# Expert mixtures: the down product turned around, with rounded splits for the sample tokens and four column groups for the prompt tokens

## The reference

```python
def expert_choice_moe(h, w_router, w_gate, w_up, w_down):
    ...
    gates, idx = lax.top_k(aff.T, cap)
    xe = t[idx]
    hid = jax.nn.silu(jnp.einsum('ecd,edf->ecf', xe, w_gate)) * jnp.einsum('ecd,edf->ecf', xe, w_up)
    ye = jnp.einsum('ecf,efd->ecd', hid, w_down) * gates[..., None].astype(h.dtype)
    out = jnp.zeros_like(t).at[idx.reshape(-1)].add(ye.reshape(-1, d))
```

## Time and profile before

| | us |
|---|---|
| median of 3 runs | 4536.19 (4535.85 to 4536.8) |
| the profiled execution, its own time | 4531.31 |
| its span, first to last instruction | 4529.7 |
| PE busy in the span | 3930.1 (87%) |
| the three product groups of the mixtures (lines 1390 and 1413), PE busy | 524.4 + 517.5 + 515.6 |

### The profile page before, as it was taken

The page is one execution under the profiler, slowest core; times in us unless marked ns, Lnnn a source line. Parts: engine busy times, 40 slices in busy tenths (PEclk is TensorE's granted clock), DMA queues, the critical chain, the costliest instruction groups (busy, mean ns, idle before and its releaser), DMA issues. The chain is left out here.

```text
span 4529.7 us, 63871 instructions
## 1 busy us (share of the span) xinstructions
PE 3930.1 (87%) x25037; PEld 3363.6 (74%) x25037; DVE 1418.3 (31%) x2316; ACT 918.4 (20%) x1867; POOL 532.1 (12%) x560
## 2 busy tenths in 40 slices
PE   8689999986899999995999996688599359999996
PEld 1468989864499999994999992344355359999996
DVE  0233433335311111112203437688543531111111
ACT  1223333322110111103222220233221201111111
POOL 0000000020000100002110016333200000001100
PEclk9799999987899999995999998899799579999998
DMA  6200000035688778852212238433432447887775
GB/s 233 77 13 10 8 9 8 4 108 220 237 278 281 269 246 279 279 167 78 78 52 78 79 96 358 166 125 125 186 143 93 163 166 246 279 278 276 261 258 195
DMA packets 351387, 736.85 MB, mean 163 GB/s; under 512 B 24381, under 2 KB 78098, under 8 KB 338642
## 3 DMA queue, kind: packets, MB, share of 16 engines
q1 hardware_dynamic: 315728, 627.98, 38.6%
q0 software_dynamic: 21920, 73.15, 5.8%
q10 hardware_dynamic: 13666, 34.74, 2.0%
HBM read 636.83 MB, written 98.99 MB: 162 GB/s over the span
## 5 line engine op out<-in xcount | busy, mean ns | idle before, releaser
L1390 PE MATMUL banks<-moe_xT,mix_wg 128*128 128x144 f32 x4096 | 524.4, 288 | 5.5 <-DVE moe_xT L1459 1.9
L1390 PEld LDWEIGHTS banks<-moe_xT,mix_wg 128*128 128x128 f32 x4096 | 511.6, 191 | 13.8 <-issue 13.7
L1390 PE MATMUL banks<-moe_xT,mix_wu 128*128 128x144 f32 x4096 | 517.5, 286 | 0.0
L1413 PE MATMUL banks<-moe_hid,moe_wd 128*128 128x144 f32 x4096 | 515.6, 287 | 2.0 <-DVE moe_hid L1466 2.0
L1390 PEld LDWEIGHTS banks<-moe_xT,mix_wu 128*128 128x128 f32 x4096 | 508.2, 190 | 0.0
L1413 PEld LDWEIGHTS banks<-moe_hid,moe_wd 128*128 128x128 f32 x4096 | 505.3, 190 | 3.8 <-DVE moe_hid L1466 2.4
L1466 DVE TENSOR_TENSOR moe_hid<-moe_sg,banks 128x432 f32<-128x432 f32 (+1 forms) x96 | 53.2, 554 | 950.9 <-ACT moe_sg L1437 950.9
L1437 ACT ACTIVATE moe_sg<-banks 128x432 f32<-128x432 f32 (+1 forms) x96 | 47.1, 490 | 903.6 <-PE banks L1390 903.6
L1329 POOL DMA_INDIRECT res<-moe_y_s,moe_id_s x32 | 51.9, 1622 | 1396.7 <-DVE moe_y_p L1478 1396.7
L97 PE MATMUL banks<-h_hi,conv_w_hi 128*128 128x384 f32 x576 | 195.0, 339 | 11.6 <-DVE conv_w_lo L1851 10.8
L1473 DVE TENSOR_TENSOR moe_ye<-banks,modc 128x384 f32<-128x384 f32 (+1 forms) x192 | 59.7, 352 | 449.5 <-PE banks L1413 449.5
(11 more groups left out here) (354 smaller groups left out, 6559.1 us busy)
## 6 DMA issues: line engine op xcount, KB each, us to landing
mix_wg<-in_moe_w_gate SPq DMA_DIRECT2D x64, 2048.0 KB, 7.9
mix_wu<-in_moe_w_up SPq DMA_DIRECT2D x64, 2048.0 KB, 12.9
moe_wd<-in_moe_w_down SPq DMA_DIRECT2D x64, 2048.0 KB, 9.2
start_m_w<-in_w_mod SPq DMA_DIRECT2D x12, 2048.0 KB, 9.5
topk_m_w<-in_w_mod SPq DMA_DIRECT2D x12, 2048.0 KB, 9.2
states_x<-d_xs SPq DMA_DIRECT2D x18, 1024.0 KB, 9.8
d_hin<-states_h ACTq DMA_DIRECT2D x18, 1024.0 KB, 8.0
ssd_hin<-d_hin SPq DMA_DIRECT2D x18, 1024.0 KB, 9.8
```

Of the source, the lines that this page charges most:

```text
L1390: last = pe.matmul(PS[:, bank, CAP * (f - a):CAP * (f - a + 1)], w[:, f // 4, k, P * (f % 4):P * (f % 4) + P], xT[:, k, :], start=(k == 0) ...
L1413: last = pe.matmul(PS[:, q, CAP * (f - a):CAP * (f - a + 1)], wd[:, f // 4, k, P * (f % 4):P * (f % 4) + P], hid[:, k, :], start=(k == 0), ...
```

## The change

Only the down product and what hangs on it change; gate and up stay. Per expert:

- The down product is turned around: activations are stationary and weights move, so the result has tokens on partitions at once, and `rows_back` and `ye` go.
- Sample tokens: 48 matmuls by `exact_products`, 512 columns moving, two banks. ACT rounds the down weights into `wd_hi` (`rounded_down`, four pieces of 128x2048) and the hidden values into `hid_hi`; POOL makes `wd_lo` (`rest_of_down`, four pieces, between its gather and its scatter), DVE makes `hid_lo` (`rest_of_hidden`).
- Prompt tokens: 32 float32 matmuls (eight contraction steps, four column groups `j`). The stationary operand is the 16 tokens, held twice (32 columns); group `j` writes PSUM partitions 32j to 32j + 31 with 256 of the 1024 output features.
- The gates are multiplied in when DVE empties PSUM, from `g2s` and `g2p`, which ten matmuls make once per layer.
- Prompt rows travel as 128 pieces of 512 B in place of 16 rows of 4 KB; `choose` makes their indices with nine more small DVE operations. One transpose replaces the eight small ones.
- `y_s` now lies in `sg`, `y_2` in `hid_p`. The down weights of the next expert are loaded once the prompt products have read them (`p_mm`) and POOL has made the remainders (`dlo_ok`).
- The bias of the modulation is loaded by SP inside `Modulation`, once per layer, in place of ACT at the start.

```diff
+        rows_p = st.sb("rows_p", [NE, KD, CAP_P])
...
+                for k in range(KD):
+                    dve.tensor_scalar(rows_p[:, k], rows[:, CAP_S:CAP], float(KD), float(k), ALU.mult, ALU.add).then_inc(picked, 1)
...
         wd = st.sb("wd", [P, 2, KD, HB])
+        wd_hi, wd_lo = st.sb("wd_hi", [P, 2, KD, HB], F32R), st.sb("wd_lo", [P, 2, KD, HB], F32R)
...
-        x_p = st.sb("x_p", [CAP_P, D])
+        x_p = st.sb("x_p", [P, P])
...
+        id_p = st.sb("id_p", [P, 2], U32)
...
         sg = st.sb("sg", [P, KD, CAP])
-        hid = st.sb("hid", [P, KD, CAP])
-        ye = st.sb("ye", [P, KD, CAP])
-        y_s = st.sb("y_s", [P, D])
-        y_p = st.sb("y_p", [CAP_P, D])
+        hid_hi, hid_lo = st.sb("hid_hi", [P, KD, CAP_S], F32R), st.sb("hid_lo", [P, KD, CAP_S], F32R)
+        hid_p = st.sb("hid_p", [P, KD, 2, CAP_P])
+        y_s = sg[:].rearrange("p k c -> p (k c)")[:, 0:D]
+        y_2 = hid_p[:].rearrange("p k u c -> p (k u c)").rearrange("p (i n) -> p i n", i=2)
+        y_p = st.sb("y_p", [P, P])
+        g2s = st.sb("g2s", [P, D])
+        g2p = st.sb("g2p", [P, 2, P])
...
+        normed_p = g.normed.rearrange("t (k p) -> (t k) p", p=P)
+        res_p = g.res.rearrange("t (k p) -> (t k) p", p=P)
...
-                        sp.wait_ge(half_d if half == 0 else d_mm, e if half == 0 else 3 * e)
+                        sp.wait_ge(p_mm, e)
+                        sp.wait_ge(dlo_ok, 4 * e - 2 + 2 * half)
                         load_down(e, half)
...
-                    pool.indirect_dma_start(x_p[:], None, g.normed, bass.IndirectOffsetOnAxis(ap=id_p[:, 0:1], axis=0),
...
+                    pool.indirect_dma_start(x_p[:], None, normed_p, bass.IndirectOffsetOnAxis(ap=id_p[:, 0:1], axis=0),
...
-                    wait_alone(pool, ys_ok, 2 * e + 2)
-                    pool.indirect_dma_start(g.res, bass.IndirectOffsetOnAxis(ap=id_s[:, 1:2], axis=0), y_s[:], None,
+                    wait_alone(pool, ys_ok, 2 * e + 3)
+                    pool.indirect_dma_start(g.res, bass.IndirectOffsetOnAxis(ap=id_s[:, 1:2], axis=0), y_s, None,
...
                     wait_alone(pool, yp_ok, e + 1)
...
+                                            bounds_check=KD * T - 1, compute_op=ALU.add).then_inc(yp_out, 16)
+                def rest_of_down(e):
+                    for n in range(4):
+                        half, ks = n // 2, slice(4 * (n % 2), 4 * (n % 2) + 4)
+                        wait_alone(pool, dhi_ok, 4 * e + n + 1)
+                        pool.tensor_tensor(wd_lo[:, half, ks], wd[:, half, ks], wd_hi[:, half, ks].bitcast(F32),
+                                           ALU.subtract).then_inc(dlo_ok, 1)
...
                         gather(e + 1, 4 * e + 2)
+                        rest_of_down(e)
                         scatter(e, 4 * e + 4)
                     else:
+                        rest_of_down(e)
                         scatter(e, 4 * e + 2)
...
+                    pe.transpose(PS[:, 3, 0:P], x_p[:], g.ident[:]).then_inc(x_mm, 1)
+                pe.sem_inc(d_mm, 1)
+                pe.wait_ge(g2_in, 3)
+                for k in range(KD):
+                    pe.matmul(PS[:, k // 4, P * (k % 4):P * (k % 4) + P], sg[:, k, 0:P], g.ident[:], start=True, stop=True)
+                picks = hid_p[:].rearrange("p k u c -> p (k u c)")
...
+                tokens(0, 0)
...
+                            if bank < 2:
+                                pe.wait_ge(ys_ok, 2 * e + bank)
...
-                        tokens(e + 1, 2 * e, 3 * e + 1)
+                        tokens(e + 1, 3 * e + 1)
                     pe.wait_ge(hid_ok, 3 * e + 3)
-                    for q, (a, b) in enumerate(TRIOS):
...
+                    for half in range(2):
+                        pe.wait_ge(wd_in[half], 16 * e + 16)
+                    for k in range(KD):
+                        for j in range(4):
+                            last = pe.matmul(PS[32 * j:32 * j + 32, 4, 0:256], hid_p[:, k].rearrange("p u c -> p (u c)"),
+                                             wd[:, j // 2, k, 256 * (j % 2):256 * (j % 2) + 256],
+                                             start=(k == 0), stop=(k == KD - 1))
+                    last.then_inc(p_mm, 1)
+                    pe.wait_ge(hlo_ok, 3 * e + 3)
+                    for half in range(2):
+                        for k in range(KD):
+                            if k % 4 == 0:
+                                pe.wait_ge(dlo_ok, 4 * e + 2 * half + k // 4 + 1)
+                            last = exact_products(pe, PS[:, half, :], (hid_hi[:, k], hid_lo[:, k]), (wd_hi[:, half, k], wd_lo[:, half, k]),
+                                                  k == 0, k == KD - 1)
                         last.then_inc(d_mm, 1)
...
+                def rounded_down(e, half):
+                    act.wait_ge(wd_in[half], 16 * e + 16)
+                    act.wait_ge(d_mm, 2 * e + half)
+                    for k0 in (0, 4):
+                        act.copy(wd_hi[:, half, k0:k0 + 4], wd[:, half, k0:k0 + 4]).then_inc(dhi_ok, 1)
+                def rounded_hidden(e, q):
+                    a, b = TRIOS[q]
+                    act.wait_ge(hid_ok, 3 * e + q + 1)
+                    act.copy(hid_hi[:, a:b], sg[:, a:b, 0:CAP_S]).then_inc(hhi_ok, 1)
                 tokens(0)
                 def body(e, more):
                     for q, (a, b) in enumerate(TRIOS):
+                        if q < 2:
+                            rounded_down(e, q)
                         act.wait_ge(gu_mm, 3 * e + q + 1)
+                        if q == 0:
+                            act.wait_ge(ys_out, 16 * e)
                         act.activation(sg[:, a:b], trio(q, a, b), ACT.Silu).then_inc(sg_ok, 1)
+                        if q:
+                            rounded_hidden(e, q - 1)
+                    rounded_hidden(e, 2)
                     if more:
                         tokens(e + 1)
...
-                        act.activation(y_s[:, 512 * half:512 * half + 512], PS[:, 6 + half, :], ACT.Copy,
-                                       scale=g.gate_s[:, bass.ds(e, 1)]).then_inc(ys_ok, 1)
...
+                gates = g.modc[:, layer, 40:48]
+                dve.sem_inc(ys_ok, 1)
+                dve.tensor_copy(sg[:, :, 0:P], gates[:, :, 1:2].to_broadcast([P, KD, P])).then_inc(g2_in, 1)
...
+                dve.wait_ge(g2_mm, 1)
+                dve.tensor_copy(g2s[:].rearrange("p (t n) -> p t n", t=2), PS[:, 0:2, :]).then_inc(g2_ok, 1)
+                dve.tensor_copy(g2p[:], PS[:, 2, 0:2 * P].rearrange("p (i n) -> p i n", i=2)).then_inc(g2_ok, 1)
...
                 tokens(0)
+                def rest_of_hidden(e, q):
+                    a, b = TRIOS[q]
+                    dve.wait_ge(hhi_ok, 3 * e + q + 1)
+                    dve.tensor_tensor(hid_lo[:, a:b], sg[:, a:b, 0:CAP_S], hid_hi[:, a:b].bitcast(F32), ALU.subtract).then_inc(hlo_ok, 1)
                 def body(e, more):
                     for q, (a, b) in enumerate(TRIOS):
                         dve.wait_ge(sg_ok, 3 * e + q + 1)
-                        dve.tensor_tensor(hid[:, a:b], sg[:, a:b], trio(3 + q, a, b), ALU.mult).then_inc(hid_ok, 1)
+                        up = trio(3 + q, a, b)
+                        dve.tensor_tensor(hid_p[:, a:b], sg[:, a:b, CAP_S:CAP].unsqueeze(2).to_broadcast([P, b - a, 2, CAP_P]),
+                                          up[:, :, CAP_S:CAP].unsqueeze(2).to_broadcast([P, b - a, 2, CAP_P]), ALU.mult)
+                        dve.tensor_tensor(sg[:, a:b, 0:CAP_S], sg[:, a:b, 0:CAP_S], up[:, :, 0:CAP_S], ALU.mult).then_inc(hid_ok, 1)
+                        if q:
+                            rest_of_hidden(e, q - 1)
+                    rest_of_hidden(e, 2)
                     if more:
                         tokens(e + 1)
-                    for q, (a, b) in enumerate(TRIOS):
...
-                                              ALU.mult).then_inc(ye_ok, 1)
...
+                    dve.wait_ge(p_mm, e + 1)
+                    dve.scalar_tensor_tensor(out=y_2, in0=PS[:, 4, 0:2 * P].rearrange("p (i n) -> p i n", i=2),
+                                             scalar=g.gate_p[:, bass.ds(e, 1)], in1=g2p[:], op0=ALU.mult, op1=ALU.mult).then_inc(y2_ok, 1)
...
                     dve.wait_ge(yp_out, 16 * e)
...
-                                      g.gate_p[:, bass.ds(e, 1)], None, ALU.mult).then_inc(yp_ok, 1)
+                    dve.tensor_tensor(y_p[:], y_2[:, 0], y_2[:, 1], ALU.add).then_inc(yp_ok, 1)
+                    dve.wait_ge(ys_out, 16 * e)
+                    for half in range(2):
+                        dve.wait_ge(d_mm, 2 * e + half + 2)
+                        c = slice(HB * half, HB * half + HB)
+                        dve.scalar_tensor_tensor(out=y_s[:, c], in0=PS[:, half, :], scalar=g.gate_s[:, bass.ds(e, 1)],
+                                                 in1=g2s[:, c], op0=ALU.mult, op1=ALU.mult).then_inc(ys_ok, 1)
```

(18 more changed lines are left out.)

80 lines of the change are left out of this document (27 added, 53 removed).

## The result

The changed kernel takes 4425.12 us (median of 4 runs, 4421.04 to 4427.07) against 4536.49 us: a ratio of 0.9753, with an interval of 0.9741 to 0.9765. The forecast was no change, 4538 us, so it was wrong, and the time lies 3 us outside the range too. What happened is rival 1, which had put 4438 us.

What follows compares the result with a forecast made beforehand. The tensor engine's queue was taken as the bound; the new tail's terms, 1.37 + 7.2 + 10.9 + 0.1 = 19.6 us against 19.56 a turn, plus 1 us once per layer, gave 4538 us, range 4428 to 4570.

Steps and rivals of the forecast that it cites:

- rival 1: Prompt matmuls: all four column groups stream at once, 4.1 us in place of 7.2, 4438 us in all; chance 0.30.
- (b): The 32 prompt matmuls: two records side by side at most, one record's time per matmul, 7.2 us a turn.
- The lower bound: Prompt matmuls: the issue rate, 0.064 us a record, so 64 records need at least 4.1 us.
- (c): The 48 rounded products of 512 columns: 0.227 us each as in the attention's output, 10.9 us a turn.
- (a): From the start of the token transposes until the down product may begin: 1.37 us, against 1.57 before.
- (d): The edge from one turn of the expert loop to the next: 0.1 us.
- Once per layer: Gate matmuls, index operations in `choose`, last evacuation and bias loads: together about +1 us, bounds -3 to +5.
- Rival 3: Prompt matmuls: weight loads are not covered, 10.2 us for the block, 4633 us in all; chance 0.06.
- Rival 4: Down-weight remainders: POOL is late, a turn grows by up to 1 us, up to 4570 us; chance 0.06.
- partial overlap: The prediction's own case for the prompt matmuls: two streams at most, 4524 to 4552 us; chance 0.44.
- full overlap: Prompt matmuls of all four column groups stream at once, 4438 us; chance 0.30.

Runs made afterwards that it cites:

- runs: The changed kernel with the prompt matmuls ordered by column group, all sixteen records of a group in a row: 4675.3 us.
- half_turns: The changed kernel with the prompt product on bfloat16 views, one record per matmul instead of two: 4342.6 us.
- ahead: The changed kernel with `hid_hi` and `hid_lo` allocated ahead of `wd` in SBUF instead of behind it: 4414.2 us.
- one_group: The changed kernel with all 32 prompt matmuls in column group 0, three quarters of the prompt result not computed: 4755.1 us.

## Why the prediction was wrong

- **(b), the prompt block: the step that failed.** "so the second has to wait for the first, and the next group's first record stands behind it." The second does wait, but in its own group's queue, and the next group's first record starts past it. That "a record starts when the one ahead has streamed" was read from rows in which all matmuls went to the same columns; there it could not be otherwise, and it said nothing on other groups. 3.59 us instead of 7.2 is 116 us over 32 turns, a little more than the whole miss of 113 us (4538 − 4425). The Trainium skill, TensorE: Matmul & The Clock Gate, Part 3, has matmuls of different tiles start in the order of the program; in runs group 1's first record starts beside group 0's thirteenth, ahead of group 0's last three, so the measurement decides against it. The four times of the Trainium skill, TensorEngine Tiling (Array Packing), Theoretical Speedup, are what came: 3.9.
- **The lower bound** of 4.1 us was above what happened. It took the distance of small transposes, 0.064 us, for an issue rate; in half_turns records come every 0.115 / 4 = 0.029 us. Rival 1, priced by it, came out 0.5 us a turn too slow.
- **(c), mis-sized:** 11.30 us instead of 10.9, 13 us in all. 0.3 us of it is the pitch, 48 x 0.2334 = 11.2: the `wo_` rows were of the right form, but here the place of the activations in SBUF counts, and ahead brings the pitch to 0.2272 us. The other 0.1 us is the first product, which the next follows after 0.33 us.
- **(a)** 1.25 instead of 1.37 us, from two DVE operations of 0.22 and 0.41 us, as worked out, but the second starts 0.08 us before the first ends. The 0.08 us for the semaphore came from no row; here the product starts 0.06 us after DVE ends. **(d)** nothing instead of 0.1. **Once per layer** +1 us was forecast, up to +5; in the profiled executions 5.5 us are lost outside the loops.
- **Rival 3** had no part: in the block a set comes every 0.216 us, which is the streaming time alone. Only at its end 0.33 us go from the last set to the first rounded product, and much the same, 0.31 us, goes there in one_group. **Rival 4** neither: POOL was done at 27 us, as predicted, although the down loads took 15.4 us from issue to landing and not 12.9. Up to the first rounded product, at 36.2 us of the turn, that leaves the 9 us of cover that the prediction had. The cover that counts is 5.4 us: the prediction saw that DVE's first remainder may stick behind POOL, but priced POOL's lateness by the rounded products alone.
- **The chances.** 0.44 on partial overlap and 0.30 on full overlap rested on no row that had two column groups. Neither had the better evidence, and a forecast of "no change" came from one inference that happened to cancel the gain.

## What to carry to other kernels

Float32 matmuls whose stationary operand is 32 columns wide, put into four column groups, ran four at a time here: issue them so that no group gets more than four records in a row (two float32 matmuls), and the block costs about a quarter. Where DVE works on two SBUF operands, count it as closed for the length of each GpSimd subtraction that it meets, and judge GpSimd's cover by that DVE work, not by its own consumer. Evidence on order from one column group is no evidence on two.

## What was not expected of the hardware

- A column group takes four float32 records, one streaming and three waiting: 3.66, 8.10 and 11.43 us for 4, 8 and 16 records of a group in a row, against 3.59 for 2.
- The place of the stationary tile in SBUF changes the pitch of a 512-column rounded product: 0.2334 us with both parts of the activations behind the down weights, 0.2272 with both ahead.
